# Attention's value product in three passes of halves, routing marks on GpSimd, and the expert table in two parts

## The reference

```python
v = (kv @ w_uv).reshape(B, S, H, DV)
s = jnp.where(allowed[None, None], s, NEG_INF)     # blocks of 64 keys, causal by block
p = jax.nn.softmax(s, axis=-1).astype(v.dtype)
return jnp.einsum('bqhk,bkhd->bqhd', p, v)
# routing
e_sel = jnp.take_along_axis(e_logits, g_idx[:, None, None], axis=1)[:, 0]
top_v, top_i = lax.top_k(e_sel, TOP_K)
gates = jax.nn.softmax(top_v, axis=-1) * p_group[:, None]
expert = g_idx[:, None] * EXPERTS_PER_GROUP + top_i
# each expert works on its tokens; the results are weighted and added
```

## Time and profile before

| what | value |
|---|---|
| runs | 2059.62, 2056.75, 2064.39 us; median 2059.62 |
| the profiled execution | 2057.8 us, its span 2056.0 us |
| granted clock, mean | 0.953 |
| PE busy | 1855.8 us (90% of the span) |
| DVE busy | 1285.5 us (63%) |
| ACT busy | 694.9 us (34%) |
| POOL busy | 484.5 us (24%) |
| value product, L899, PE | 640 records of all widths, busy 292.6 us |
| exponential, L1113, ACT | 320, busy 170.2 us |
| reciprocal, L992, DVE | 132, busy 124.3 us |

### The profile page before, as it was taken

One profiled execution on the slowest core, in us unless ns is written; L12 is line 12 of the kernel. 1 busy time (PEld: TensorE's weight loads), 2 busy tenths in 40 slices (PEclk: granted clock), 3 DMA queues, 4 the chain that ended last, 5 costly groups with the idle time before them and its releaser, 6 DMA issues. The chain is left out here.

```text
span 2056.0 us, 27000 instructions
## 1 busy us (share of the span) xinstructions
PE 1855.8 (90%) x8674; PEld 1441.8 (70%) x8674; DVE 1285.5 (63%) x2171; ACT 694.9 (34%) x1106; POOL 484.5 (24%) x540
## 2 busy tenths in 40 slices
PE   2999999987999999999996999973999999999980
PEld 2677878764666666666654788862899999999960
DVE  5688888856786786786785655645344444444444
ACT  2545353324444444444443233220222221212114
POOL 0131413112221221221221111100234343434330
PEclk9999999997999999999998999986999999999995
DMA  7655656510000000000003444414699999999958
GB/s 273 203 177 150 201 139 179 147 54 0 9 8 6 8 8 6 8 8 6 8 8 131 144 153 149 145 64 154 215 274 268 279 271 276 268 279 271 276 109 327
DMA packets 213570, 290.81 MB, mean 141 GB/s; under 512 B 23829, under 2 KB 167408, under 8 KB 213242
## 3 DMA queue, kind: packets, MB, share of 16 engines
q1 hardware_dynamic: 190906, 220.60, 32.6%
q0 software_dynamic: 20224, 69.22, 13.5%
q10 hardware_dynamic: 2368, 0.17, 0.1%
HBM read 229.13 MB, written 60.82 MB: 141 GB/s over the span
## 5 line engine op out<-in xcount | busy, mean ns | idle before, releaser
L899 PE MATMUL tbank<-probs,VV 128*128 128x512 f32 (+3 forms) x640 | 292.6, 538 | 1.2 <-ACT probs L1113 1.2
L1113 ACT ACTIVATE probs<-tbank 128x512 f32<-128x512 f32 (+1 forms) x320 | 170.2, 532 | 248.5 <-PE tbank L870 243.5
L981 DVE TENSOR_REDUCE cmax<-tbank 128x1 f32<-128x512 f32 (+2 forms) x340 | 204.2, 601 | 74.8 <-PE tbank L824 68.6
L1854 DVE TENSOR_SCALAR xTe<-ebank,modcol 128x256 f32<-128x256 f32 (+1 forms) x128 | 53.8, 472 | 261.2 <-PE ebank L1774 138.5
L381 PE MATMUL pbank<-hhi,wslhi 128*128 128x512 f32 x512 | 206.9, 404 | 7.2 <-DVE wsllo L432 6.5
L868 PE MATMUL tbank<-Qhi,Khi 97*128 97x512 f32 (+2 forms) x321 | 212.5, 662 | 0.0
L381 PE MATMUL pbank<-hhi,wsllo 128*128 128x512 f32 x512 | 201.3, 393 | 0.0
L381 PE MATMUL pbank<-hlo,wslhi 128*128 128x512 f32 x512 | 201.0, 393 | 0.0
L1139 POOL TENSOR_SCALAR diag<-cst,nmax 128x128 fp32r<-128x128 f32 x138 | 84.1, 610 | 492.2 <-DVE nmax L984 491.9
L1796 PE MATMUL ebank<-xTe,wg 128*128 128x192 f32 x1024 | 173.2, 328 | 3.1 <-DVE ahi L1882 1.8
L1796 PEld LDWEIGHTS ebank<-xTe,wg 128*128 128x128 f32 x1024 | 169.2, 191 | 7.9 <-DVE ahi L1882 2.1
(11 more groups left out here) (271 smaller groups left out, 3482.2 us busy)
## 6 DMA issues: line engine op xcount, KB each, us to landing
wg<-in_w_exp_gate SPq DMA_DIRECT2D x32, 1024.0 KB, 6.6
wu<-in_w_exp_up SPq DMA_DIRECT2D x32, 1024.0 KB, 9.9
wd<-in_w_exp_down SPq DMA_DIRECT2D x32, 1024.0 KB, 7.6
wraw<-in_w_in SPq DMA_DIRECT2D x60, 512.0 KB, 4.1
wmod<-in_w_ada POOLq DMA_DIRECT2D x64, 256.0 KB, 3.4
wada<-in_w_ada SPq DMA_DIRECT2D x2, 4096.0 KB, 20.2
xt<-in_x SPq DMA_DIRECT2D x4, 2048.0 KB, 12.4
mixed<-mix_dram SPq DMA_DIRECT2D x16, 512.0 KB, 4.3
```

The costliest lines, as they stand in the source:

```text
L899: ins = pe.matmul(out, VV[:, kt, 2 * b:2 * b + 2].rearrange("p c d -> p (c d)"), step_of(probs, m), start=kt == 0, stop=last)
L981: W(ve.tensor_reduce(cmax[:, i % 2, n:n + 1], plain[:, chunk % 2, 0:w], AX.X, ALU.max), plain_read)
L1113: A(act.activation(step_of(probs, m), scores[:, m % 2, j * P:512], ACT.Exp), exp_done)
```

## The change

**attend.** Values and probabilities are split into a high half (F32R) and a low half. ACT makes two exponentials of each score: `phi`, rounded to F32R, and `probs` in F32; POOL subtracts (`prob_low`) and gives `plo`. The value product becomes VVhi phi, VVlo phi and, two steps later (LAG), VVhi plo (`value_low`). `phi`, `plo` and `probs` are rings of four; `probs` lies over `KR`, so ACT's loop waits for DVE's last read of it (`rope_rest`). DVE makes VVlo (`lower_values`). The copy of the sums moves to step kt = 2 and puts the two halves of the columns on partitions 0 to 63 and 64 to 127, in four ACT operations; so the division is two reciprocals of 128 x 128 and a multiplication of 128 x 256, and each group is stored by two DMAs. The ones, zeros and first fills come from ACT in place of POOL and DVE, and PE waits for seven of them.

**route.** POOL makes all marks but the first gate part, beside DVE: three operations for each of the two picks, and after `gates_split` four more. The mask of `em` is one operation in place of two.

**experts.** `inslot` is built in two parts (slots 0 to 127, then the rest). PE first multiplies the two token marks (64 columns), three groups of 32, then the other four marks (128 columns), two groups. DVE makes both index lists first; POOL waits for these two before the first gathers and for the other two after them.

```diff
@@ -700,14 +700,15 @@
 V_PARTS = NT // 4
-V_AT = [(1, STEPS_HEAD - NT + 4 * (v + 1)) if v < V_PARTS - 1 else (0, 1) for v in range(V_PARTS)]
+LAG = 2
+RING = 4
+V_AT = [(1, STEPS_HEAD - NT + 4 * (v + 1) + LAG) if v < V_PARTS - 1 else (0, LAG + 1) for v in range(V_PARTS)]
...
-DIVIDE_AT = {m: (g, r) for g, steps in ((GROUPS - 1, (6, 7, 8, 10)), (0, (12, 13, 14, 16)),
-                                        (1, (18, 19, 20, 22)), (2, (28, 29, 30, 31)))
+DIVIDE_AT = {m: (g, r) for g, steps in ((GROUPS - 1, (6, 7)), (0, (12, 13)), (1, (18, 19)), (2, (29, 30)))
@@ -725,14 +726,13 @@
-        VV = sb("VV", [P, NT, 4, VD])
-        probs = sb("probs", [P, 4 * 512])
+        VVhi, VVlo = sb("VVhi", [P, NT, 4, VD], F32R), sb("VVlo", [P, NT, 4, VD], F32R)
+        phi, plo = sb("phi", [P, RING, 512], F32R), sb("plo", [P, RING, 512], F32R)
+        probs = KR[:].rearrange("p (r n) -> p r n", r=RING)
...
-        rs, on = sb("rs", [VD, 512]), sb("on", [VD, 2, 512])
-        raw = sb("raw", [P, 2, 512])
+        rs, on = sb("rs", [P, 256]), sb("on", [P, 2, 256])
+        raw = sb("raw", [P, 2, 2, 256])
@@ -780,9 +779,9 @@
+            sp.sem_inc(plo_done, RING)
@@ -790,10 +789,13 @@
                         sp.wait_ge(divided, hp * 2 * GROUPS + (b * GROUPS + g + 4))
-                        sp.dma_start(mix_dram[VD * b:VD * (b + 1), bass.ds(hp, 1), g * 512:(g + 1) * 512],
...
+                        for h in range(2):
+                            sp.dma_start(mix_dram[VD * b:VD * (b + 1), bass.ds(hp, 1),
+                                                  g * 512 + h * 256:g * 512 + (h + 1) * 256],
+                                         on[h * VD:(h + 1) * VD, (g + 1) % 2:(g + 1) % 2 + 1]
+                                         ).then_inc(stored[(g + 1) % 2], 16)
@@ -874,10 +876,24 @@
             pe.wait_ge(rope_rest, 1)
-            pe.wait_ge(filled, 2)
-            pe.wait_ge(v_copied, V_EARLY)
+            pe.wait_ge(filled, 7)
+            pe.wait_ge(v_lowered, V_EARLY)
...
+            def value_low(m, b, first):
+                g, kt = STEP_OF[m]
+                last = kt == GQ * (g + 1) - 1
+                pe.wait_ge(plo_done, first + (m + 1 + RING))
+                ins = pe.matmul(outp[:, g % 2, first_tile(g, kt) * P:512], heads_values(VVhi, kt, b),
+                                step_of(plo, m), start=False, stop=last)
+                if last:
+                    ins.then_inc(out_done, 1)
@@ -885,21 +901,17 @@
-                        ins = pe.matmul(out, VV[:, kt, 2 * b:2 * b + 2].rearrange("p c d -> p (c d)"),
-                                        step_of(probs, m), start=kt == 0, stop=last)
...
+                        pe.matmul(out, heads_values(VVhi, kt, b), step_of(phi, m), start=kt == 0, stop=False)
+                        pe.matmul(out, heads_values(VVlo, kt, b), step_of(phi, m), start=False, stop=False)
@@ -930,13 +944,21 @@
                         value(m)
+                        if m >= LAG:
+                            value_low(m - LAG, b, hp * 2 * STEPS_HEAD + b * STEPS_HEAD)
+                        else:
+                            value_low(m - LAG + STEPS_HEAD, 1 - b, hp * 2 * STEPS_HEAD + (b - 1) * STEPS_HEAD)
@@ -984,17 +1006,23 @@
+            def lower_values(v, pair, src=made):
+                ve.wait_ge(v_copied, pair * V_PARTS + (v + 1))
+                at = slice(v * 4, (v + 1) * 4)
+                W(ve.tensor_tensor(VVlo[:, at, 0::2], src.rearrange("p (t c d) -> p t c d", c=2, d=VD),
+                                   VVhi[:, at, 0::2].bitcast(F32), ALU.subtract), v_lowered)
...
-                W(ve.reciprocal(rs[:, r * P:(r + 1) * P], raw[VD:P, g % 2, r * P:(r + 1) * P]))
-                if r == 3:
+                W(ve.reciprocal(rs[:, r * P:(r + 1) * P], raw[:, g % 2, 1, r * P:(r + 1) * P]))
+                if r == 1:
...
-                    W(ve.tensor_tensor(on[:, p], raw[0:VD, g % 2], rs[:], ALU.mult), divided)
+                    W(ve.tensor_tensor(on[:, p], raw[:, g % 2, 0], rs[:], ALU.mult), divided)
@@ -1018,16 +1046,18 @@
+                if 0 < n <= V_EARLY:
+                    lower_values(n - 1, 0, bank[:, V_EARLY_BANK[n - 1]])
...
-            W(ve.memset(outp[:, 1], 1.0), out_set)
@@ -1039,13 +1069,15 @@
                             part(PART_AT[m], 1 - b, hp * 2 + (b + 1))
+                        if (b, m - 1) in V_AT:
+                            lower_values(V_AT.index((b, m - 1)), hp + b)
@@ -1076,7 +1108,11 @@
                 act.wait_ge(divided, head * GROUPS + (g + 2))
-                A(act.activation(raw[:, g % 2], outp[:, g % 2], ACT.Copy), out_free)
+                for h in range(2):
+                    half = slice(h * VD, (h + 1) * VD)
+                    act.activation(raw[half, g % 2, 0], outp[0:VD, g % 2, h * 256:(h + 1) * 256], ACT.Copy)
+                    ins = act.activation(raw[half, g % 2, 1], outp[VD:P, g % 2, h * 256:(h + 1) * 256], ACT.Copy)
+                A(ins, out_free)
@@ -1098,20 +1134,30 @@
                 mask_rows(0, n)
+                v, k = (VVhi, VVlo)[n % 2], n // 2 * 2 + 1
+                A(act.activation(v[:, :, k], cst[:, C_ONE:C_ONE + VD].unsqueeze(1).to_broadcast([P, NT, VD]), ACT.Copy,
+                                 scale=1.0 - n % 2), filled)
+            for k in (0, 2):
+                A(act.activation(VVhi[:, NT - LAG:, k], cst[:, C_ONE:C_ONE + VD].unsqueeze(1).to_broadcast([P, LAG, VD]),
+                                 ACT.Copy, scale=0.0), filled)
+            A(act.activation(plo[:, RING - LAG:].rearrange("p r (a n) -> p (r a) n", n=P),
+                             cst[:, C_ONE:C_ONE + P].unsqueeze(1).to_broadcast([P, LAG * 4, P]), ACT.Copy, scale=0.0), filled)
...
-            act.wait_ge(out_set, 1)
+            act.wait_ge(rope_rest, 2)
...
+                        act.wait_ge(plo_done, hp * 2 * STEPS_HEAD + (b * STEPS_HEAD + m + 1))
+                        A(act.activation(step_of(phi, m), scores[:, m % 2, j * P:512], ACT.Exp), phi_done)
...
-                        if kt == 0:
+                        if kt == LAG:
@@ -1139,18 +1185,21 @@
                                  nmax[:, i:i + 1], None, ALU.mult).then_inc(diag_ready, 1)
+            def prob_low(m, count):
+                hold(po, exp_done, count, passed_pool)
+                po.tensor_tensor(step_of(plo, m), step_of(probs, m), step_of(phi, m).bitcast(F32), ALU.subtract
+                                 ).then_inc(plo_done, 1)
...
-                if n == 0:
...
-                        po.memset(VV[:, :, k], 1.0).then_inc(filled, 1)
...
+                        prob_low(m, hp * 2 * STEPS_HEAD + (b * STEPS_HEAD + m + 1))
@@ -1535,6 +1585,27 @@
+        def gate_marks(i, k):
+            return (marks[:, :, k, (3 + i) * NEXP:(4 + i) * NEXP], pick[:, :, k],
+                    across(gpart[:, i, k::2].unsqueeze(2), NT, NEXP), ALU.mult)
+        @block.gpsimd
+        def _(po):
+            for k in range(2):
+                po.wait_ge(picked[k], 1)
+                po.tensor_tensor(marks[:, :, k, 0:NEXP], pick[:, :, k],
+                                 cst[:, C_SLOT:C_SLOT + NT].unsqueeze(2).to_broadcast([P, NT, NEXP]), ALU.mult
...
+                po.tensor_scalar(marks[:, :, k, 2 * NEXP:3 * NEXP], pick[:, :, k], float(1 + k), None, ALU.mult
...
+                po.tensor_scalar(marks[:, :, k, NEXP:2 * NEXP], pick[:, :, k], cst[:, C_PART:C_PART + 1], None, ALU.mult
...
+            po.wait_ge(gates_split, 1)
+            for i in (1, 2):
+                for k in range(2):
+                    po.tensor_tensor(*gate_marks(i, k)).then_inc(marked, 1)
+            po.wait_ge(marked, 10)
@@ -1556,15 +1627,14 @@
-            do(ve.tensor_tensor(in_groups(em[:]), in_groups(E), on_experts(gone[:]), ALU.mult))
-            do(ve.tensor_tensor(in_groups(em[:]), in_groups(em[:]), on_experts(gpen[:]), ALU.add))
+            do(ve.tensor_tensor(in_groups(em[:]), in_groups(E), on_experts(gpen[:]), ALU.min))
@@ -1573,7 +1643,7 @@
-                do(ve.tensor_tensor(pick[:, :, k], cand[:], across(low[:], NT, NEXP), ALU.is_equal))
+                do(ve.tensor_tensor(pick[:, :, k], cand[:], across(low[:], NT, NEXP), ALU.is_equal), picked[k])
@@ -1587,19 +1657,12 @@
-            for k in range(2):
-                do(ve.tensor_tensor(marks[:, :, k, 0:NEXP], pick[:, :, k],
...
-                do(ve.tensor_copy(gpart[:, i], left if i else gates[:]))
+                do(ve.tensor_copy(gpart[:, i], left if i else gates[:]), gates_split if i == 2 else None)
...
-                for k in range(2):
-                    do(ve.tensor_tensor(marks[:, :, k, (3 + i) * NEXP:(4 + i) * NEXP], pick[:, :, k],
...
+            for k in range(2):
+                do(ve.tensor_tensor(*gate_marks(0, k)))
@@ -1739,11 +1802,12 @@
             with po.Fori(0, n_rounds) as r:
-                hold(po, table_ready, r * 4 + 4, passed_pool)
+                hold(po, table_ready, r * 4 + 2, passed_pool)
...
```

(38 more changed lines are left out.)

86 lines of the change are left out of this document (37 added, 49 removed).

## The result

The changed kernel takes 2082.52 us (median of 4 runs, 2081.72 to 2083.45), the kernel before 2060.74 beside it. The ratio is 1.011, 95% interval 1.0096 to 1.0123: slower by 22 us, where 2030 was forecast (range 2012 to 2047). The profiled execution has a span of 2081.7 us at a mean granted clock of 0.938 (before: 2056.0 at 0.953).

What follows compares the result with a forecast made beforehand. PE was taken to bound the attention. From 2057.8 us: -32 value product, +10 stalls, +5 start, -0.5 behind the last head, -4 route, -6 slots and table gave 2030.3, said as 2030; range 2012 to 2047.

Steps and rivals of the forecast that it cites:

- Contention: In attention, DVE operations with two SBUF inputs meet POOL's subtractions: 8 a head, about 0.6 us each, 5 us a head.
- all three places: Attention: POOL's diagonals, ACT's quarter copies at a head's start, DVE's bunched operations; PE stalls 10 us in all, bounds 0–40.
- one meeting: Query addition before the change: 0.68 us alone, 1.13 us when it met POOL's subtraction and waited for its end.
- Next late: In attention, the plain score would be late after DVE's operations; it may run at most two steps ahead of DVE.
- the value product: Attention on PE: three F32R passes replace one F32 product, full step 1.80 to 1.66 us; saves 32 us, 28 to 38.
- the route: Routing: marks moved from DVE to POOL shorten DVE's chain; -4 us, bounds -7 to +1.
- the table: Slots and expert table: index lists ready 6 us earlier, and the gathers with them; -6 us, bounds -3 to -7.
- the start: Before attention: ACT waits for DVE's last Klo subtraction and gets fills, so the first exponential comes 5 us later (2 to 9).
- POOL becomes the bound: Rival: in attention, POOL's in-order queue idles at diagonals waiting for DVE's maximum; about 2081 us, chance 0.05.
- The forecast's own sign of being wrong: Even step stays at 1.8 us, or PE idles over 25 us before score weight loads or late passes; releaser names the rival.
- Half is given back: Rival: DVE's blocked operations hold plain scores at divisions and query parts, 3 us a head, 24 us: 2044, chance 0.13.

Runs made afterwards that it cites:

- run 7: Changed kernel with last value part back at step 26, ACT's loop written out, and query addition reading one operand from PSUM: 2031.20 us, ratio 0.9864.
- run 6: Changed kernel with the turned half written back into PSUM, so query additions have one SBUF operand; POOL keeps its work: 2056.79 us, ratio 0.9985.
- run 1: Changed kernel without POOL's 320 subtractions; the third pass reads phi again, so the low half is lacking: 2049.16 us, ratio 0.9947.
- run 3: Changed kernel with the last value part of a pair moved from step 3 to step 26, behind the queries: 2062.38 us, ratio 1.0003.
- run 5: Changed kernel with ACT's loop over the four pairs of heads written out: 2079.15 us, ratio 1.0099.
- run 9: Changed kernel with last value part at step 26 and query addition with one PSUM operand, ACT's loop left a loop: 2035.61 us, ratio 0.9893.
- run 8: Changed kernel without POOL's subtraction, with last value part at step 26 and ACT's loop written out; third pass reads phi: 2028.45 us, ratio 0.9859.
- run 2: Changed kernel with POOL waiting for the end of each of its subtractions before the next instruction: 2090.04 us, ratio 1.0153.

## Why the prediction was wrong

**The step that failed** is the one under Contention, "I charge 1.2 us of PE stalls a head for all three places, 10 us in all", and with it the cost of order that no step priced. With the three causes mended (run 7) the kernel takes 2031, with them 2082.5: beside the 10 us charged stand 51 us that no term held.

- **The volume of contention was right, its bunching wrong.** I charged DVE 8 x 0.6 = 5 us a head. Measured: additions 47.6 - 32 x 0.683 = 25.7 us over their own work, multiplications 37.5 - 33 x 0.425 = 23.5, together 6.2 us a head. But I took from one meeting that a meeting costs the rest of one POOL operation. There POOL had nothing behind it but a fill, which reads nothing (its row is below), and the addition ended at 456.41, beside it. In the loop operations that read SBUF stand behind, and one addition a head waits 3.2 us at a stroke. PE's lead of two chunks, some 1.6 us a step, covers 0.6 but not 3.2. It cost 25.7 us by run 6, and 33.4 by run 1, which frees the multiplications as well.

```profile
455.82 1.95 POOL L1146 MEMSET VV<- 128x1024 f32 x2
```

- **Next late, and the clock.** I named the plain score as the next thing to be late, and it was. What I did not price is what follows a stop of 2 us: a stretch at the lower clock level. Each of the eight stops cost 25.7 / 8 = 3.2 us with 1.9 us of idle, each of the four at the keys 5.0 with 1.9.
- **A moved step.** V_AT was in the diff: the last value part goes from step 1 to step 3, behind the keys of step 2 in the same PSUM bank. I listed the edit nowhere. 20.1 us by run 3, almost as much as the starved addition.
- **The loop's turn.** ACT's loop body grew with 40 exponentials a head (1532 ACT instructions in the profile after). It restarts 2.2 us late and then loads its table, where before the load was nearly all there was. 3 to 4 us by runs 5, 7 and 9, with overlapping intervals in 5 and 9. The profile of before showed the table load at each turn and DVE's restart; I did not look at a boundary at all. Why the restart is longer, by the length of the body or otherwise, was not tried.
- **Right:** the value product (step 1.63 for 1.66); the route (-4.5 for -4); the table (-4.4 for -6: the index lists won 8.0 for the 6 forecast, and the first gathers, now beside the experts' weight loads, took 12.3 us for 8.6); the start (+2.5 for +5). Runs 7 and 8 are the forecast's sum without its missing steps: attention 599 and 591 us for the 590 written (the forecast's own terms, 617.7 - 32 + 10 - 0.5, give 595), 2031 and 2028 in all for 2030. That 2031 meets 2030 is partly luck: by its trace run 7 gains 18.7 in the attention and loses 3.2 at the start, and its span is 29.5 shorter than before. So 14.1 us were won behind the last copy of a sum, of which the rows of route and table explain 8.9. That part takes 952.8 us before the change and 938.7 to 945.9 in the ten traces that have the changed route and table; run 7 has the shortest. The other 5 us are no more than this part varies by with the same code.
- **The rivals.** "POOL becomes the bound", 2081, came nearest in time and had the wrong mechanism: POOL was 72% busy, and with all of its work kept the time fell by 51 us. Its volume binds only when gaps are forced (run 2). The forecast's own sign of being wrong came true (PE idle for 37 us against the 25 named), and the first releaser's name, DVE, pointed to the next rival. "Half is given back" had the right engine and the right victim (DVE's blocked operations hold the plain scores), at 24 us; it lacked the 3.9 us wait, the slow matmuls behind a stop and the moved part.

**Open:** what is left between run 7 and a kernel with no stall (13.6 us of waits, of which 4.9 stand behind DVE's restart); what moving the division's multiplication off SBUF operands gains (some 2.6 us by the traces of runs 1 and 6, as an estimate). And a stream without a gap is not enough for such a wait. In the routing POOL makes six marks in a row without a gap, from 1421.83 to 1431.12, and DVE's operations with two SBUF inputs get in between:

```profile
1425.26 1.56 POOL L1602 TENSOR_SCALAR marks<-pick,cst 128x512 bf16<-128x512 f32 x1
1425.69 0.79 DVE L1646 TENSOR_TENSOR pick<-cand,low 128x512 f32<-128x512 f32 x1
```

This one takes 0.79 us for 0.69, and the longest delay in that stretch is 0.7 us. Why DVE gets in there and not in the attention was not tried.

## What to carry to other kernels

When POOL gets a dense stream, look at each DVE operation that has two SBUF inputs, and let the upper bound of its price be not one meeting but the longest run of that stream without a gap, at the step with the least slack; the cure here was an operand in PSUM, not less work. Count every step that a diff moves and every PSUM bank that it then shares, and read the boundary of a hardware loop by itself. Price a stop of PE of 2 us at about twice its idle: here stops that idled PE for 22.5 us cost 45.8, with a stretch at the lower clock behind them.

## What the runs showed of the hardware

- A DVE addition with both inputs in SBUF waited 3.2 us for four consecutive POOL operations, not for the one that it met, eight times in the changed kernel; with a wait of POOL on its own result in between it never waited more than 1.0 us; with one operand in PSUM never at all (689 ns, 32 times). A multiplication got in where POOL's operations were 0.04 us apart (523.94 to 525.40, POOL's next at 525.15). Beside POOL's bf16 marks in the routing, also without a gap, DVE operations were late by 0.7 us at most.
- Stops of 1.9 to 2.0 us of PE cost 3.2 to 5.0 us in the time, with matmuls 0.42 us apart behind them instead of 0.23.
- At the turn of its loop ACT stood 2.2 us and loaded its table (1.28 us) every time (before the change 0.17 us at most, and the same load); DVE stood 3.1 to 3.2 us in both kernels. With the loop written out ACT did neither.
- POOL's marks on 128x512 with bf16 output took 1.3 to 1.9 us, more than the 1.27 of a float32 subtraction and the 1.0 estimated, and DVE's two gate marks 2.14 for 1.42.
